# Expert weights of a two-layer backbone in longer runs: one transfer each for gate and up, 8 KB runs for down

## What is computed

```python
def hier_moe(h, w_rg, w_re, w_gate, w_up, w_down):
    ...
    xs = h[tok]
    a = lax.ragged_dot(xs, w_gate, sizes)        # 1024 -> 512
    u = lax.ragged_dot(xs, w_up, sizes)
    y = lax.ragged_dot(jax.nn.silu(a) * u, w_down, sizes)
    y = y * w.reshape(-1)[order][:, None].astype(y.dtype)
    return jax.ops.segment_sum(y, tok, num_segments=n)
```

## Time and profile before

| what | us |
|---|---|
| median of 3 runs | 5001.29 |
| lowest and highest run | 5000.02 and 5009.46 |
| span of the profiled execution | 5002.1 |
| stretch of layer 0's jobs (first to last gate product's start) | 1927.34 to 2552.08 |
| stretch of layer 1's jobs | 4244.45 to 4925.15 |

### The profile page before, as it was taken

How to read it: one execution, slowest core, us unless ns; L and a number is a source line. 1 busy time by engine, 2 the same in 40 slices (tenths; PEclk the granted TensorE clock), 3 DMA queues, 4 the chain that set the end, 5 groups by cost and what they waited for, 6 DMA issues and landing times. The chain is left out here.

```text
span 5002.1 us, 75983 instructions
## 1 busy us (share of the span) xinstructions
PE 4544.4 (91%) x25973; PEld 3776.1 (75%) x25973; DVE 3310.6 (66%) x5272; ACT 2464.5 (49%) x3056; POOL 1192.3 (24%) x921
## 2 busy tenths in 40 slices
PE   6999998889999897999967999999999987999995
PEld 4887877777877875877745878888877866788774
DVE  6653667676776567777777626677756436877776
ACT  3223555564233315777743225655633222777774
POOL 3650004400000013333334620043000001333333
PEclk8999999999999998999988999999999998999998
DMA  5645234264554566999995635253556345999998
GB/s 188 206 120 122 65 87 104 100 185 139 209 201 168 207 210 262 397 397 397 397 357 169 199 113 117 63 124 97 136 191 217 113 167 174 388 397 397 397 397 330
DMA packets 581798, 1088.92 MB, mean 218 GB/s; under 512 B 111876, under 2 KB 265380, under 8 KB 578552
## 3 DMA queue, kind: packets, MB, share of 16 engines
q1 hardware_dynamic: 531952, 919.40, 54.8%
q0 software_dynamic: 36272, 119.42, 6.6%
q10 hardware_dynamic: 13400, 47.85, 2.4%
HBM read 903.12 MB, written 183.43 MB: 217 GB/s over the span
## 5 line engine op out<-in xcount | busy, mean ns | idle before, releaser
L1800 PE MATMUL merge_acc<-ahead_wide,merge_w_split 128*128 128x512 f32 (+1 forms) x2880 | 638.7, 377 | 20.5 <-DMA ahead_wide<-hT 14.9
L1800 PEld LDWEIGHTS merge_acc<-ahead_wide,merge_w_split 128*128 128x128 f32 x2880 | 505.4, 190 | 128.6 <-issue 18.7
L648 PE MATMUL project_proj_acc<-ahead_wide,project_hT 128*128 128x512 f32 x2280 | 562.1, 399 | 3.0 <-DVE ahead_wide L471 1.7
L2502 DVE TENSOR_TENSOR experts_w_gate<-experts_raw_gate,experts_w_gate 128x2048 fp32r<-128x2048 f32 x146 | 363.4, 2495 | 295.8 <-ACT experts_w_gate L2398 295.8
L648 PEld LDWEIGHTS project_proj_acc<-ahead_wide,project_hT 128*128 128x128 f32 x2280 | 426.1, 191 | 94.0 <-DVE project_hT L501 4.6
L2377 POOL TENSOR_TENSOR experts_w_down<-experts_raw_down,experts_w_down 128x2048 fp32r<-128x2048 f32 x73 | 355.9, 4876 | 512.5 <-ACT experts_w_down L2398 512.5
L2549 PE MATMUL experts_gate_acc<-experts_w_gate,experts_rowsT 128*128 128x512 f32 x1752 | 432.2, 403 | 13.2 <-DVE experts_rowsT L2507 6.9
L964 DVE TENSOR_REDUCE attend_stat<-attend_scores 128x1 f32<-128x1280 f32 (+2 forms) x288 | 305.7, 1061 | 205.9 <-PE attend_scores L865 202.2
L2563 PE MATMUL experts_result_acc<-experts_w_down,experts_hiddenT 128*128 128x512 f32 x1752 | 430.1, 401 | 12.2 <-DVE experts_w_down L2502 12.2
L2549 PE MATMUL experts_up_acc<-experts_w_up,experts_rowsT 128*128 128x512 f32 x1752 | 420.6, 395 | 0.0
L2549 PEld LDWEIGHTS experts_gate_acc<-experts_w_gate,experts_rowsT 128*128 128x128 f32 x1752 | 327.0, 190 | 101.5 <-issue 22.0
(11 more groups left out here) (257 smaller groups left out, 8298.5 us busy)
## 6 DMA issues: line engine op xcount, KB each, us to landing
experts_raw_gate<-in_w_exp_gate_dram SPq DMA_DIRECT2D x146, 1024.0 KB, 13.8
experts_raw_up<-in_w_exp_up_dram SPq DMA_DIRECT2D x146, 1024.0 KB, 12.8
experts_raw_down<-in_w_exp_down_dram SPq DMA_DIRECT2D x146, 1024.0 KB, 11.4
ahead_rows<-in_w_merge_dram SPq DMA_DIRECT2D x120, 768.0 KB, 6.4
merge_mod_w_ada<-in_w_ada_rows_dram POOLq DMA_DIRECT2D x80, 512.0 KB, 3.7
qk<-project_staged SPq DMA_DIRECT2D x74, 512.0 KB, 3.4
ye<-ahead_rows ACTq DMA_DIRECT2D x73, 512.0 KB, 6.3
attend_keys<-qk SPq DMA_DIRECT2D x96, 320.0 KB, 5.6
```

Source lines behind the costliest of these rows:

```text
L648: m = pe.matmul(acc[g % 2][:, :], hT[:, a, q * KP + k, t * P:(t + 1) * P], w_split[n % SLOTS][:, c, k, :], start=(q == 0 and i == 0 and k ...
L1800: m = pe.matmul(acc[:, b, 0:w], w_split[b][:, a, k, :], hT[:, x, k, 0:w], start=(i == 0 and k == 0), stop=(i == 2 and k == KD - 1))
L2502: dve.tensor_tensor(w[n][:, 1, half, :], raw[n][:, half, :], w[n][:, 0, half, :].bitcast(F32), ALU.subtract).then_inc(w_lo[n].sem, 1)
```

## The change

Gate and up each come in one transfer of 2 MB instead of two of 1 MB. The arrays in DRAM are laid out anew ahead of the launch (`by_partition`), so that each partition's 16 KB of gate or up, and 8 KB of each half of down, are contiguous. The transfer into a raw buffer then has one run of 16 KB per partition for gate and up, and one of 8 KB for a half of down. The load of gate and up waits until both halves of the job before are split; ScalarE waits once, ahead of the first half's cast, for the whole matrix. What stands in a raw buffer, its casts, splits and products are as before.

```diff
@@ -1994,9 +1994,8 @@
             if nq > NL:
                 body(NL // 2, 1)
             for n in range(2):
-                for half in range(2):
-                    sp.dma_start(raw[n][:, half, :], expert_half(io, l, slice(0, 1), n, half)
-                                 ).then_inc(raw_in[n][half].sem, 16)
+                sp.dma_start(raw[n][:, :, :].rearrange("p h n -> p (h n)"), expert_matrix(io, l, slice(0, 1), n)
+                             ).then_inc(raw_in[n][0].sem, 16)
 
         @block.gpsimd
         def _(pool):
@@ -2256,7 +2255,12 @@
 
     w = io[("w_exp_gate", "w_exp_up", "w_exp_down")[n]]
     rows = w.shape[2] // 2
-    return w[l, e, half * rows:(half + 1) * rows, :].rearrange("o (k p) n -> p (o k) n", p=P)
+    return w[l, e, half * rows:(half + 1) * rows, :].rearrange("o (p k) n -> p (o k n)", p=P)
+
+
+def expert_matrix(io, l, e, n):
+
+    return io[("w_exp_gate", "w_exp_up")[n]][l, e, :, :].rearrange("o (p k) n -> p (o k n)", p=P)
 
 
 def run_experts(nc, io, scr, l, nq, st, inner, ident, jobs, starts, more_jobs, r, scat, raw, raw_in,
@@ -2334,6 +2338,11 @@
 
             def load(n, g):
                 e = sp.value_load(jobs[0:1, ds(g, 1)], min_val=0, max_val=NE - 1)
+                if n != DOWN:
+                    wait_split(sp, n, 1, g - 1)
+                    sp.dma_start(raw[n][:, :, :].rearrange("p h n -> p (h n)"), expert_matrix(io, l, ds(e, 1), n)
+                                 ).then_inc(raw_in[n][0].sem, 16)
+                    return
                 for half in range(2):
                     wait_split(sp, n, half, g - 1)
                     sp.dma_start(raw[n][:, half, :], expert_half(io, l, ds(e, 1), n, half)
@@ -2394,7 +2403,8 @@
                 if later(g, 1):
                     act.wait_ge(products[n].sem, products[n].done(g - 1))
                 for half in range(2):
-                    act.wait_ge(raw_in[n][half].sem, raw_in[n][half].done(g))
+                    if n == DOWN or half == 0:
+                        act.wait_ge(raw_in[n][half].sem, raw_in[n][half].done(g))
                     act.copy(w[n][:, 0, half, :], raw[n][:, half, :]).then_inc(w_hi[n].sem, 1)
 
             def rows_hi(g):
@@ -2677,7 +2687,16 @@
     w_ada = [np.asarray(w).T.reshape(N_MOD * KD, P, D) for w in np.asarray(inputs["w_ada"])]
     b_ada = [np.asarray(b).reshape(N_MOD * KD, P) for b in np.asarray(inputs["b_ada"])]
     two = 2 * KD
-    return {"w_ada_rows0": np.concatenate([w_ada[0][two:], w_ada[1][:two]]), "w_ada_rows1": w_ada[1][two:],
+
+    def by_partition(name, parts):
+        w = np.asarray(inputs[name])
+        rows, n = w.shape[2:]
+        pieces = w.reshape(DEPTH, NE, parts, rows // (parts * P), P, n).transpose(0, 1, 2, 4, 3, 5)
+        return np.ascontiguousarray(pieces).reshape(DEPTH, NE, rows, n)
+
+    return {"w_exp_gate": by_partition("w_exp_gate", 1), "w_exp_up": by_partition("w_exp_up", 1),
+            "w_exp_down": by_partition("w_exp_down", 2),
+            "w_ada_rows0": np.concatenate([w_ada[0][two:], w_ada[1][:two]]), "w_ada_rows1": w_ada[1][two:],
             "b_ada_columns0": np.concatenate([b_ada[0][two:], b_ada[1][:two]]).T, "b_ada_columns1": b_ada[1][two:].T,
             "c_rows": np.concatenate([np.asarray(inputs["c"]).reshape(1, D), np.asarray(inputs["c_ctx"]).reshape(1, D)]),
             "w_router": np.ascontiguousarray(router.reshape(DEPTH, KD, P, NG + NE).transpose(0, 2, 1, 3)),
```

## The result

| | us |
|---|---|
| before, median of 4 runs beside it | 5001.99 (5000.02 to 5009.46) |
| after, median of 4 runs | 5100.28 (5096.01 to 5113.53) |
| ratio | 1.0201, 95% interval 1.0188 to 1.0213 |
| profiled execution of after, its span | 5101.2 |

The change costs 2%, where 4983 us, 0.4% less, was forecast; the range ended at 5050.

What follows compares the result with a forecast made beforehand. The prediction took the DMA engines to bound the experts' stage, with TensorE next: 5002.1 - 21 (TensorE's pace) + 3 (lost at layer starts) = 4984.1 us of profiled span, 4983 against the median; range 4975 to 5050.

Steps and rivals of the forecast that it cites:

- What bound the kernel: Experts' stage: DMA engines set the later jobs' pace, about 18.49 us each, TensorE's 18.11 us next; 21 us to gain.
- Price of the packets: Weight loads: 16 KB packets at 0.61 us, 8 KB at 0.31, so DMA needs 16.8 to 17.5 us a job.
- (4): Gate and up loads: 16 KB packets take 0.96 us, 22.2 us a job, 5253 us in all; chance 0.05.
- (5): Weight loads: runs cut short again or memory holds 397 GB/s, 18.48 us a job stays, 5004 us; chance 0.08.
- Turns: Row gather beside loads: each of 8 packets per engine lets one 16 KB packet pass, at most 4.2 us more.
- Rival (3): DMA queues: an engine finishes all 8 packets of a transfer before switching, 19.5 us a job, 5076 us; chance 0.03.
- The slack of the gather: From the gather's landing to the transposes that read its rows: 5.6 us, so 4.2 us more would fit.
- Growth of the round: Index and gather: 0 to 1 us more wait ahead of the first packet, besides 4.2 us of turns.
- The whole-matrix wait: Gate and up casts: a chain 2.6 us longer, paid once per layer; gate lands by 21 where 27.6 would do.
- Rival (2): Index and gather: wait ahead of small packets grows with packet size, two-job loop, 19.8 us a job, 5093 us; chance 0.14.

Runs made afterwards that it cites:

- e5: Kernel before with down alone in runs of 8 KB, gate and up as before; 4991.99 us, ratio 0.9982.
- e9: Kernel before with gate and up in runs of 4 KB, still in two transfers of 1 MB each; 4986.47 us, ratio 0.9960.
- e3: Changed kernel with the next job's index fetched into a second buffer while this job's rows are gathered; 4992.06 us, ratio 0.9983.
- e2: Changed kernel's whole 2 MB transfers and waits, but runs as before, 2 KB for gate and up, 4 KB for down; 5052.28 us, ratio 1.0072.
- e12: Changed kernel with its whole transfers of gate and up in runs of 4 KB, down in 8 KB; 5057.37 us, ratio 1.0113.
- e13: Changed kernel with gate and up whole in runs of 4 KB and the next index fetched ahead; 5008.75 us, ratio 1.0012.
- e11: Kernel before with gate and up in halves in runs of 4 KB and the next index fetched ahead; 4989.58 us, ratio 0.9968.
- e1: Kernel before, its transfers in halves and waits kept, with all weight runs 8 KB; 5033.98 us, ratio 1.0069.
- e10: Kernel before with each job's index fetched three times in a row, no packet changed; 5513.42 us, ratio 1.1019.

## Why the prediction was wrong, step by step

- **What bound the kernel: right.** With the DMA engines relieved and nothing else touched (e5, e9) the job goes to 18.3 and 18.1 us. The forecast's 4984 us for its own span is what e9 shows, 4986.4.
- **Price of the packets: right.** 16 KB took 611 ns at the median (0.61 was taken, 0.96 feared), 8 KB 309; the mean of 16 KB, 674, is higher, and at 18.1 us a job the share is 0.99 (e3), so there is less room than the 0.6 to 1.3 us worked out. Rivals (4) and (5) fell.
- **Turns: right in kind, too small.** 4.2 us at most were priced; the landing grew by 4.7 at the median, and by 5.3 in the 17 rounds that wait for it. Two things besides long load packets are in that: the whole transfer (e2: 9.2 us with packets as before), and the store, some 70 of whose packets now begin between the first and the last of a gather's 128, where none did (packet records, means in 2071 to 2552 us). Rival (3) fell: a gather's packets are spread over 6.0 us, with some 120 load packets begun among them (137 over 2.2 us before), and don't pass in one turn.
- **The slack of the gather: wrong, and this is the step that failed.** 5.6 us were measured from the landing to the transposes that read the rows. But GpSimd waits for the same landing sooner, ahead of the next index fetch. The rows for it stood there: an index fetch at 1939.66 that had been held for 7.13 us by the gather's landing, and index issued 4345.39, gather issued 4351.23, landing 7.0 later, with 1.3 to the next fetch: 5.84 + 7.0 + 1.3 = 14.1 us, 4.0 under 18.11. The growth that the prediction itself priced, 4.2 and 0 to 1, would not have fit.
- **Growth of the round: under-summed.** In the 17 rounds that wait for the landing, the gather grew by 5.3 us and the index by 1.0 (0 to 1 was taken): 6.3 against 4.0, which makes 20.4 us of the 18.1. With the seven rounds that don't wait the mean is 19.4, about the 19.55 us a job. The longer issue of the gather (0.99 to 1.59 us) had no term; it lies within the landing, and what it may add is in the last section.
- **The whole-matrix wait: wrong.** It was priced at 2.6 us once per layer, since gate "lands by about 21, where 27.6 would do". Each landing delays the next request, so the bound is per round: 18.1 - 6.6 = 11.5 us from request to landing, 24.7 in the text's count, and the landing was put at 5 us plus the rest of down, some 8, where e12 has 12.6. The rest of down, gather and store all pass before it. In the changed kernel the other round hides this; e12 shows it: 53 us over the kernel before and 71 over the same runs in halves (e9); with the index ahead some 20 are left (e13 against e11).
- **Rival (2)** gave 19.8 us a job and 5093 us, which is near, but by another mechanism: it had the wait ahead of the first small packet grow by 3 us and 1.9 more on the index, on a loop of two jobs. By the packet records the gather's first packet starts 4.30 us after its issue begins in the kernel before and 4.41 in the changed one (means in 2071 to 2552 us): that wait hardly grew, though in e1 it is 5.21. The loop is of one job (e10).

## What to carry to other kernels

Before making transfers longer, write down every round that closes through a semaphore (request, landing, use, next request), each with its whole length from the trace, and compare it with the pace that is to come; slack to the consumer is not the slack of the round. A queue that shares engines with long packets sees its small transfers land later the longer these packets are, so give it a second buffer to take serial steps apart, or choose the shortest run that frees the engines, here 4 KB. Merging two transfers into one also takes away the overlap between using the first half and reloading it.

## What the runs showed of the hardware

The gather's issue on GpSimd takes 0.97 to 1.00 us in 69 of 73 jobs of the kernel before and 2.0 to 2.85 in the other four, the only ones in which one of VectorE's weight splits (a subtraction of two operands in SBUF) was running when it began and for 0.9 us on. In the changed kernel, whose jobs drift, a split was running so at 33 of 73 issues, 2.42 us at the mean (1.76 to 3.10) against 1.13 for the others. A gather with such an issue also lands later: with an issue of over 1.7 us after 12.8 us at the mean in the changed kernel, with a shorter one after 10.3; in e9, where TensorE never waits for it, 10.6 and 7.9 (both stretches of the earlier trace rows). So splits that fall on the issue may be a part of the gather's growth, which would fit the uneven jobs; that the one causes the other was not tried. The Trainium skill, page "SBUF — State Buffer", section "Who interferes with whom", says that a VectorE instruction with two SBUF inputs contends with a GpSimd instruction that reads SBUF; the gather reads its index there, and the trace agrees. The reverse case shows as well: VectorE's gate splits, every second of which now runs beside GpSimd's down split, take 3285 ns at the mean instead of 2390 (groups of 2071 to 2552 us, before and changed).

```profile
L2502 DVE TENSOR_TENSOR experts_w_gate<-experts_raw_gate,experts_w_gate 128x2048 fp32r<-128x2048 f32 x52 | 124.3, 2390 | 113.3 <-ACT experts_w_gate L2398 113.3
```

```profile
L2512 DVE TENSOR_TENSOR experts_w_gate<-experts_raw_gate,experts_w_gate 128x2048 fp32r<-128x2048 f32 x50 | 162.4, 3285 | 59.1 <-ACT experts_w_gate L2408 59.1
```
